# The last output turn of an expert moved behind the first weight piece of the next one, through two PSUM banks in turn

## What is computed

```python
    gates, idx = lax.top_k(affin.T, cap)
    xs = xt[idx]
    hid = jax.nn.silu(jnp.einsum('ecd,edf->ecf', xs, w_gate)) * jnp.einsum('ecd,edf->ecf', xs, w_up)
    y = jnp.einsum('ecf,efd->ecd', hid, w_down) * gates[..., None].astype(xt.dtype)
    out = jnp.zeros_like(xt).at[idx.reshape(-1)].add(y.reshape(-1, shp[-1]))
```

## Time and profile before

| what | us |
|---|---|
| median of 3 runs (lowest, highest) | 3696.39 (3690.32, 3703.71) |
| the profiled execution, its own time | 3681.82 |
| span of the profiled execution | 3680.0 |
| first matmul work of expert 0 begins at about | 1937 |
| from one scatter of an expert to the next one's | 104.06 |
| last scatter starts at | 3604.47 |

### The profile page before, as it was taken

One profiled execution on the slowest core, in us unless ns is written; L12 is line 12 of the kernel. 1 busy time (PEld: TensorE's weight loads), 2 busy tenths in 40 slices (PEclk: granted clock), 3 DMA queues, 4 the chain that ended last, 5 costly groups with the idle time before them and its releaser, 6 DMA issues.

```text
span 3680.0 us, 52503 instructions
## 1 busy us (share of the span) xinstructions
PE 3337.8 (91%) x21052; PEld 3006.4 (82%) x21052; DVE 2169.9 (59%) x2375; ACT 1769.2 (48%) x1916; POOL 572.7 (16%) x611
## 2 busy tenths in 40 slices
PE   5899999997889989997759999999999999999991
PEld 4677777776768877786549999999999999999991
DVE  5634333453552245233787777777777777777774
ACT  5633433553552245223335555555555555555552
POOL 1054045002221013101210000000000000000001
PEclk9999999998999999998979999999999999999995
DMA  7765455586114411342558888888888888888876
GB/s 274 265 221 192 171 182 176 191 284 234 59 35 162 159 61 30 122 150 87 187 172 263 265 275 267 260 266 252 278 270 270 275 268 260 262 262 263 276 234 254
DMA packets 544952, 775.87 MB, mean 211 GB/s; under 512 B 16160, under 2 KB 409600, under 8 KB 536144
## 3 DMA queue, kind: packets, MB, share of 16 engines
q1 hardware_dynamic: 507072, 616.60, 50.2%
q0 software_dynamic: 37776, 157.84, 13.2%
HBM read 708.19 MB, written 66.19 MB: 210 GB/s over the span
## 4 chain that ended last, share of the span: by engine, by line
PE 75%; DVE 8%; ACT 5%; DMA 5%; POOL 4%; issue 3%; ACTq 0%; POOLq 0%; DVEq 0%
PE PS L787 29%; PE PS L789 12%; PE PS L571 12%; PE PS L743 10%; DVE wlo L1146 2%; PE PS L691 2%; ACT whi L860 1%; DMA arena_ab<-k_rope 1%; PE PS L662 1%; PE PS L710 1%; DVE lo_f L1425 1%; PE PS L518 1%; PE PS L665 1%; PE PS L678 1%; PE PS L519 1%
## 5 line engine op out<-in xcount | busy, mean ns | idle before, releaser
L787 PE MATMUL PS<-xT,hi_f 128*128 128x320 f32 x4096 | 1055.1, 346 | 0.0
L1425 DVE TENSOR_TENSOR lo_f<-raw_f,hi_f 128x2048 fp32r<-128x2048 f32 x384 | 878.9, 2289 | 255.2 <-ACT hi_f L1070 250.4
L789 PE MATMUL PS<-xT,lo_f 128*128 128x160 f32 x4096 | 965.9, 236 | 0.0
L1146 DVE TENSOR_TENSOR wlo<-raw,whi 128x2048 fp32r<-128x2048 f32 x204 | 471.8, 2330 | 661.2 <-ACT whi L860 660.7
L789 PEld LDWEIGHTS PS<-xT,lo_f 128*128 128x128 f32 x4096 | 782.3, 191 | 0.0
L1070 ACT ACTIVATE hi_f<-raw_f 128x2048 fp32r<-128x2048 f32 x384 | 733.0, 1909 | 96.9 <-PE PS L789 92.0
L787 PEld LDWEIGHTS PS<-xT,hi_f 128*128 128x128 f32 x4096 | 768.7, 188 | 0.0
L860 ACT ACTIVATE whi<-raw 128x2048 fp32r<-128x2048 f32 x204 | 387.3, 1916 | 538.9 <-PE PS L743 293.0
L787 PE MATMUL PS<-hid,hi_f 128*128 128x320 f32 x2048 | 533.7, 346 | 0.0
L789 PE MATMUL PS<-hid,lo_f 128*128 128x160 f32 x2048 | 482.8, 236 | 0.0
L789 PEld LDWEIGHTS PS<-hid,lo_f 128*128 128x128 f32 x2048 | 390.7, 191 | 0.0
(11 more groups left out here) (274 smaller groups left out, 4747.7 us busy)
## 6 DMA issues: line engine op xcount, KB each, us to landing
raw_f<-w_gate SPq DMA_DIRECT2D x128, 1024.0 KB, 4.9
raw_f<-w_up SPq DMA_DIRECT2D x128, 1024.0 KB, 5.0
raw_f<-w_down SPq DMA_DIRECT2D x128, 1024.0 KB, 5.1
raw<-w_ada SPq DMA_DIRECT2D x96, 1024.0 KB, 5.1
raw<-w_in SPq DMA_DIRECT2D x60, 1024.0 KB, 5.5
raw<-w_out SPq DMA_DIRECT2D x48, 1024.0 KB, 5.2
arena_ab<-x_sample POOLq DMA_DIRECT2D x8, 1024.0 KB, 12.0
arena_cd<-x_sample POOLq DMA_DIRECT2D x8, 1024.0 KB, 6.2
```

The costliest lines, as they stand in the source:

```text
L787: nc.tensor.matmul(PS[:, b + m, 0:2 * CAP], hi_f[:, n % NSPL_F, r, w], x, start=(kt == 0), stop=False, skip_group_check=True)
L789: ins = nc.tensor.matmul(PS[:, b + m, 0:CAP], lo_f[:, n % NSPL_F, r, w], x[:, 0:CAP], start=False, stop=(kt == last_kt), skip_group_check= ...
L1146: nc.vector.tensor_tensor(wlos[slot(n)], raws[slot(n)], whis[slot(n)].bitcast(F32), ALU.subtract).then_inc(lo_ok, 1)
L1425: nc.vector.tensor_tensor(lo_f[:, n % NSPL_F], raw_f[:, n % NRAW_F], hi_f[:, n % NSPL_F].bitcast(F32), ALU.subtract).then_inc(f_lo_ok, 1)
```

## The change

`turn_outputs(3)` of an expert leaves the end of the loop body. PE now does it in the next expert, behind the matmuls of piece 0, and once behind the loop for the last expert. The turned outputs go to bank 6 and bank 7 in turn (the context rows of the last quarter to bank 5, which had bank 7), and with that PE no longer waits for `ys_ok`, the scaling of the quarter before. Ahead of piece 0 PE waits until the sums of the down piece before the last have been read. So that the first expert has something to turn, DVE clears `yT` and `yTp` once, and all counts of `yT_ok` are eight higher, those of `y_tr` one.

```diff
-                def turn_outputs(cc):
-
-                    pe.wait_ge(yT_ok, e * 8 + 2 * cc + 2)
-                    if cc:
-                        pe.wait_ge(ys_ok, e * 4 + cc)
+                def turn_outputs(cc, e):
+
+                    pe.wait_ge(yT_ok, e * 8 + 2 * cc + 10)
                     for m in range(4):
-                        last = nc.tensor.transpose(PS[:, 6, m * P:(m + 1) * P], yT[:, cc % 2, m, :], ident[:])
+                        last = nc.tensor.transpose(PS[:, 6 + cc % 2, m * P:(m + 1) * P], yT[:, cc % 2, m, :], ident[:])
                         if cc == 3:
-                            last = nc.tensor.transpose(PS[:, 7, m * P:(m + 1) * P],
+                            last = nc.tensor.transpose(PS[:, 5, m * P:(m + 1) * P],
                                                        yTp[:, m].rearrange("p a b -> p (a b)"), ident[:])
                     last.then_inc(y_tr, 1)
 
                 n = 0
+                pe.wait_ge(yT_ok, e * 8 + 7)
...
                             last.then_inc(f_used, 1)
                             n += 1
+                            if n == 1:
+                                turn_outputs(3, e - 1)
...
                     if cc in (1, 2):
-                        turn_outputs(cc - 1)
-                turn_outputs(3)
+                        turn_outputs(cc - 1, e)
+            turn_outputs(3, NE - 1)
...
+            nc.vector.memset(yTp[:], 0.0)
+            nc.vector.memset(yT[:], 0.0).then_inc(yT_ok, 8)
...
-                    dve.wait_ge(y_tr, e * 4 + c + 1)
-                    nc.vector.scalar_tensor_tensor(out=y_s[:, s], in0=PS[:, 6, :], scalar=gate_s[:, bass.ds(e, 1)],
+                    dve.wait_ge(y_tr, e * 4 + c + 2)
+                    nc.vector.scalar_tensor_tensor(out=y_s[:, s], in0=PS[:, 6 + c % 2, :], scalar=gate_s[:, bass.ds(e, 1)],
```

More of the change, by code:

```diff
@@ L825, in _ @@
                     else:
-                        pe.wait_ge(yT_ok, e * 8 + c - 1)
+                        pe.wait_ge(yT_ok, e * 8 + c + 7)
                     pe.wait_ge(f_lo_ok, e * PIECES_E + NRAW_F + n + 1)
@@ L837, in _ @@
                     if cc == 3:
-                        turn_outputs(2)
+                        turn_outputs(2, e)
                     pe.wait_ge(h_in, e * 5 + 7 + cc)
@@ L1100, in expert_hi @@
                         if c >= 2:
-                            act.wait_ge(yT_ok, e * 8 + c - 1)
+                            act.wait_ge(yT_ok, e * 8 + c + 7)
                         nc.scalar.activation(part[:, c % 2, :].rearrange("p (a b) -> p a b", a=2),
@@ L1112, in expert_hi @@
                         split_f(n + NSPL_F - PIECES_E, e + 1)
-                act.wait_ge(yT_ok, e * 8 + 8)
+                act.wait_ge(yT_ok, e * 8 + 16)
             with act.Fori(0, NE - 1) as e:
@@ L1465, in scale_rows @@
                     s = slice(c * CC, (c + 1) * CC)
-                    dve.wait_ge(y_tr, e * 4 + c + 1)
-                    nc.vector.scalar_tensor_tensor(out=y_s[:, s], in0=PS[:, 6, :], scalar=gate_s[:, bass.ds(e, 1)],
+                    dve.wait_ge(y_tr, e * 4 + c + 2)
+                    nc.vector.scalar_tensor_tensor(out=y_s[:, s], in0=PS[:, 6 + c % 2, :], scalar=gate_s[:, bass.ds(e, 1)],
                                                    in1=g2_s[:, s], op0=ALU.mult, op1=ALU.mult).then_inc(ys_ok, 1)
                     if c == 3:
-                        nc.vector.scalar_tensor_tensor(out=y_p[:], in0=PS[:, 7, :], scalar=gate_p[:, bass.ds(e, 1)],
+                        nc.vector.scalar_tensor_tensor(out=y_p[:], in0=PS[:, 5, :], scalar=gate_p[:, bass.ds(e, 1)],
                                                        in1=g2_p[:], op0=ALU.mult, op1=ALU.mult).then_inc(yp_ok, 1)
```

## The result

The changed kernel takes 3737.65 us in the median (3728.14 to 3748.41, 4 runs) against 3693.36 us (3687.31 to 3703.71, 4 runs): the ratio is 1.0113, with an interval from 1.0075 to 1.0152. The change makes the kernel 44 us slower; the interval goes from 28 to 56 us. One of the executions of the kernel before that stand beside the experiments took 11648 us; no ratio uses it. The forecast was slower, 3725 us, range 3696 to 3752.

What follows compares the result with a forecast made beforehand. PE was taken to bound the kernel, busy 102.99 of 104.06 us per expert, with a scatter-gather chain hidden by 1.9 us slack. 15 x (1.10 + 0.75) + 1.5 = 29 us on the 3696.4 median gave 3725 us, range 3696 to 3752.

Steps and rivals of the forecast that it cites:

- The wait at the end goes: Expert boundary: PE's last transposes no longer wait for DVE's scaling; gain 1.23 us at each of 15 boundaries.
- The chain starts 2.88 us later: Last transposes, scaling, scatter, gather, second `gsum`, piece 8: starts behind piece 0, so PE waits 2.33 us at piece 8.
- The chain gets 0.75 us longer through load 8: Between scatter and gather: part of weight load 8 gets ahead of the scatter's second part, 0.75 us per boundary.
- The rival in which a whole load does: Load 8 goes entirely ahead of the scatter's second part, 2.7 us per boundary: 58 us slower, 3755; chance 0.12.
- The chain shortens because the gather meets an idle DVE: Gather's issue to DVE's modulation: landing up to 2.1 us sooner, none booked; as rival 13.5 us gained, 3683, chance 0.08.
- The sum, 15 x 1.85 + 1.5 = 29 us: Whole kernel: 1.10 plus 0.75 us at each of 15 boundaries and 1.5 us once, 29 us slower.
- the new idle time of 2.3 to 3.5 us: One new PE wait per expert from the second on, ahead of a gate piece, released by `gsum`: 2.3 to 3.5 us.
- The forecast stretch of 105.2 to 106.5 us: Time from one expert's scatter to the next: 105.2 to 106.5 us in place of 104.06.
- Once 1.5 us: One-time costs: memsets 1.3 us, idle transposes of expert 0 0.8, last scaling up to 0.65 earlier; together +1.5.
- 2.9 + 1.3 + 0.8 = 5.0: Up to the first scatter: chain start 2.88 us later, two memsets 1.3, idle transposes of expert 0 0.8.

Runs made afterwards that it cites:

- e2_two_ktiles: The changed kernel with the moved transposes behind the first two of piece 0's eight k-tiles, not all: 3686.21 us, ratio 0.9978 to the kernel before.
- e5_five_ktiles: The changed kernel with the moved transposes behind five of piece 0's eight k-tiles: 3693.77 us, ratio 1.0004 to the kernel before.
- e6_behind_piece1: The changed kernel with the moved transposes a whole piece later, behind piece 1: 3815.34 us, ratio 1.0331 to the kernel before.
- e4_filled_wait: The changed kernel with 22 extra identity transposes on PE ahead of piece 8's wait: 3717.82 us, ratio 1.0079 to the kernel before.

## Why the prediction was right, and what it missed

- *The wait at the end goes, 1.23 us.* Right. With every wait gone a stretch has 102.77 us, 1.30 less than before.
- *The chain starts 2.88 us later, a wait of 2.33 us plus what the chain gains in length stands at piece 8, released by `gsum`.* Right in place and releaser, and in size: 2.33 with the 0.2 us of the next point is 2.53, measured are 2.45. With the 0.75 that the forecast booked it would have been 3.08.
- *The chain gets 0.75 us longer through load 8.* Too much. From scatter to gather it is 15.85 us in the mean of fifteen against 15.67, so 0.2. Load 8 did come closer behind the scatter, 3.8 us (2593.00 after 2589.22), as worked out, and did not get ahead of it: from 2596 to 2598 the queue of the loads moved 0.01 MB and the scatter's 0.39. The rival in which a whole load does, at 2.7 us, is refuted.
- *The chain shortens because the gather meets an idle DVE.* The gather's second instruction did fall from 2.59 to 0.98 us, and the landing did not move (8.75 after 8.68). What decides is the first instruction, as e2_two_ktiles showed from the other side. The Trainium skill, "SBUF — State Buffer", section "Who interferes with whom", says that a DVE instruction with two inputs in SBUF, as the split is, contends with a GpSimd instruction that reads SBUF. The 2.51 us for 1.00 beside a running split agree, if the gather reads its row numbers (`ig_s`, a column in SBUF) while it is issued, which no row shows.
- *The sum, 15 x 1.85 + 1.5 = 29 us.* This is the step that was mis-sized: 44 in the medians (28 to 56), 46 between the profiled spans. The part per boundary was 2.47 us in the trace, 1.38 of idle time (1.85 had been booked) and 1.10 of PE's own work at the lower clock, for which the sum had no term. The forecast named the new idle time of 2.3 to 3.5 us and did not ask what follows idle time of PE. That the total still came near is in part luck: the 0.75 us booked for the longer chain, of which 0.2 came, stood in for part of the missing 1.10. With the right 0.2 the forecast's own sum would have been 15 x 1.30 + 1.5 = 21 us. The forecast stretch of 105.2 to 106.5 us holds for the experts at full clock (105.3 to 105.7), and the mean, 106.54, lies at its edge only through the clock. In the trace of before nothing showed it there, since 1.07 us of idle never brought the clock down; a place where PE was idle for longer stands ahead of the experts (busy 7.20 of the 37 us from 1900 to 1937, at a granted clock of 0.50) and was not drawn on.
- *Once 1.5 us.* The two memsets took 0.49 and 0.91 us, 1.4 for 1.3. Of the 46 us between the two profiled spans 6 lie ahead of the experts, where the code is the same (the first gather starts at 1916.1 for 1910.2), and are the spread of the executions. From there to the first scatter it is 6.2 us more; 2.9 + 1.3 + 0.8 = 5.0 had been worked out, of which the 2.9 come back at the end, where nothing stands behind a piece.

Left open: why the clock falls behind half of the waits of 2.1 to 2.7 us and not behind the others. Their length does not tell them apart: the stretch less its busy time is 106.65 - 104.58 = 2.07 us in the one from 2694.48, with a fall, and 105.65 - 102.99 = 2.66 us in the one from 3227.71, without.

## What to carry to other kernels

Before work is moved later to cover a wait, follow the chain that starts from it to where it next meets the busy engine, and compare its slack there (here 1.9 us) with the distance moved (2.9 us); the waits of another engine on a transfer show where such a chain hides. What stands behind a late landing in program order matters as much as when it lands: one line moved behind the sum turned 44 us of loss into 18 us of gain, and did nothing in the kernel before, where piece 8 was in time. And idle time of the matrix engine has a second price in what it computes next at the lower clock, so a new wait that replaces a shorter one is to be costed with it.

## What the runs showed of the hardware

Idle time of PE of 0.9 to 1.4 us in each expert (before, e2_two_ktiles, e5_five_ktiles) left the granted clock at 1.00 in all stretches; 2.1 to 2.7 us brought it to its lower level behind half of the waits, for a loss of 1.5 or 3.1 us; 6.3 to 6.8 us (e6_behind_piece1) did so in every expert, for 1.5 to 3.1. Filling the idle time with transposes without use kept it at 1.00 (e4_filled_wait). An indirect DMA's issue on GpSimd that comes while DVE runs a subtraction with both inputs in SBUF takes until about 0.9 us after its end, up to 3.1 us for 1.0; the landing then moved by as much as that took longer, 1.2 to 2.0 us, when it was the first of two gathers, by at most 0.3 us when it was the second. A scatter of 1.3 MB with addition, with weight loads in the other queue, took 15.1 to 16.4 us to the next work of POOL in every kernel here, however the loads were placed, and 10.8 us without loads at the end of the kernel before.
